# Copying gated products by a transfer into an fp32r tile and transposing them there with an fp32r identity

## What is computed

```python
D_MODEL = 1024; BATCH = 1; SEQ = 256; DEPTH = 2; D_FF = 2816

def swiglu_ffn(x, w_in, w_out):
    gate, up = jnp.split(x @ w_in, 2, axis=-1)
    return (jax.nn.silu(gate) * up) @ w_out

def reference(x, ...):
    for i in range(DEPTH):
        x = x + 0.5 * swiglu_ffn(rms_norm(x, ffn1_norm[i]), ffn1_w_in[i], ffn1_w_out[i])
        xn = rms_norm(x, mix_norm[i])
        ...
        x = x + y
        x = x + 0.5 * swiglu_ffn(rms_norm(x, ffn2_norm[i]), ffn2_w_in[i], ffn2_w_out[i])
    return rms_norm(x, final_norm)
```

## Time and profile before

| | before |
|---|---|
| median of 3 runs | 932.08 us (932.0 to 932.5) |
| the profiled execution | 932.27 us |
| its span, first to last instruction | 930.5 us |
| PE busy | 916.5 us, 98% |
| DVE busy / ACT busy | 525.5 us, 56% / 413.4 us, 44% |
| granted TensorE clock, mean | 0.999 of 2.4 GHz |
| HBM read | 168.63 MB, 182 GB/s |

### The profile page before, as it was taken

One profiled execution on the slowest core, in us unless ns is written; L12 is line 12 of the kernel. 1 busy time (PEld: TensorE's weight loads), 2 busy tenths in 40 slices (PEclk: granted clock), 3 DMA queues, 4 the chain that ended last, 5 costly groups with the idle time before them and its releaser, 6 DMA issues.

```text
span 930.5 us, 11397 instructions
## 1 busy us (share of the span) xinstructions
PE 916.5 (98%) x4349; PEld 764.2 (82%) x4349; DVE 525.5 (56%) x511; ACT 413.4 (44%) x452; POOL 23.6 (3%) x44
## 2 busy tenths in 40 slices
PE   8999999999999999999999999999999999999997
PEld 7888888879878888888878888888799888888885
DVE  5745455458976554453565554545678464454543
ACT  5544344446844442443444434424564263434432
POOL 1400000000000000000000000000000000000000
PEclk9999999999999999999999999999999999999999
DMA  8855646725313856476528465566284266455521
GB/s 279 295 185 181 225 145 206 259 92 189 105 46 118 289 178 207 157 255 240 182 91 267 152 205 190 180 217 213 90 304 149 91 221 231 155 207 180 181 113 46
DMA packets 126668, 170.20 MB, mean 183 GB/s; under 512 B 5237, under 2 KB 111241, under 8 KB 126632
## 3 DMA queue, kind: packets, MB, share of 16 engines
q1 hardware_dynamic: 126632, 169.70, 53.8%
HBM read 168.63 MB, written 1.05 MB: 182 GB/s over the span
## 4 chain that ended last, share of the span: by engine, by line
PE 88%; DVE 7%; ACT 2%; issue 1%; DMA 1%; POOL 0%; SPq 0%; POOLq 0%; ACTq 0%; DVEq 0%
PE ga L962 10%; PE ga L964 10%; PE ga L963 10%; PE ub L964 9%; PE ub L962 9%; PE ub L963 9%; PE acc L962 9%; PE acc L964 9%; PE acc L963 9%; DVE xs L846 3%; DVE w_lo L669 3%; PE tp L1066 2%; PE tp L1023 1%; ACT w_hi L454 1%; DMA raw<-in_ffn_w_in_dram 1%
## 5 line engine op out<-in xcount | busy, mean ns | idle before, releaser
L669 DVE TENSOR_TENSOR w_lo<-raw,w_hi 128x2048 fp32r<-128x2048 f32 (+1 forms) x154 | 349.0, 2290 | 116.2 <-ACT w_hi L454 115.6
L454 ACT ACTIVATE w_hi<-raw 128x2048 fp32r<-128x2048 f32 (+1 forms) x154 | 289.2, 1903 | 30.9 <-DMA raw<-in_ffn_w_in_dram 19.5
L962 PE MATMUL acc<-w_hi,act_hi 128*128 128x512 f32 x416 | 163.5, 393 | 0.0
L964 PE MATMUL acc<-w_hi,act_lo 128*128 128x512 f32 x416 | 162.0, 389 | 0.0
L963 PE MATMUL acc<-w_lo,act_hi 128*128 128x512 f32 x416 | 161.9, 389 | 0.0
L962 PE MATMUL ga<-w_hi,xn_hi 128*128 128x512 f32 x384 | 154.9, 403 | 0.4 <-DVE w_lo L669 0.3
L964 PE MATMUL ga<-w_hi,xn_lo 128*128 128x512 f32 x384 | 150.1, 391 | 0.0
L963 PE MATMUL ga<-w_lo,xn_hi 128*128 128x512 f32 x384 | 149.8, 390 | 0.0
L964 PE MATMUL ub<-w_hi,xn_lo 128*128 128x512 f32 x384 | 149.6, 390 | 0.0
L962 PE MATMUL ub<-w_hi,xn_hi 128*128 128x512 f32 x384 | 149.5, 389 | 0.0
L963 PE MATMUL ub<-w_lo,xn_hi 128*128 128x512 f32 x384 | 149.4, 389 | 0.0
(11 more groups left out here) (133 smaller groups left out, 585.7 us busy)
## 6 DMA issues: line engine op xcount, KB each, us to landing
raw<-in_ffn_w_in_dram SPq DMA_DIRECT2D x176, 512.0 KB, 4.8
raw<-in_ffn_w_out_dram SPq DMA_DIRECT2D x88, 512.0 KB, 4.0
raw<-in_sgu_w_in_dram SPq DMA_DIRECT2D x16, 512.0 KB, 4.5
raw<-in_ab_w_in_dram SPq DMA_DIRECT2D x12, 512.0 KB, 5.0
raw<-in_ab_w_out_dram SPq DMA_DIRECT2D x8, 512.0 KB, 3.9
raw<-in_sgu_w_out_dram SPq DMA_DIRECT2D x8, 512.0 KB, 5.4
gain<-in_ffn_norm_dram SPq DMA_DIRECT2D x4, 512.0 KB, 6.0
xres<-in_x_dram SPq DMA_DIRECT2D x2, 512.0 KB, 5.8
```

The costliest lines, as they stand in the source:

```text
L454: act.activation(w_hi[:, n % RING, o:], raw[:, n % RAW, o:], ACT.Copy).then_inc(hi_split, 1)
L669: dve.tensor_tensor(w_lo[:, n % RING, o:], raw[:, n % RAW, o:], w_hi[:, n % RING, o:].bitcast(F32), ALU.subtract).then_inc(lo_split, 1)
L962: pe.matmul(dst, s_hi, m_hi, start=start, stop=False)
L964: return pe.matmul(dst, s_lo, m_hi, start=False, stop=stop)
```

## The change

- A second identity `ident_r` of type fp32r is made once, by ACT, in the first network.
- `turn` is a pair of fp32r tiles of 128 x 512 in the slots of `act_lo` and `act_hi` that the networks leave free.
- After the two `gate_rows` of steps 0 to 9 ACT runs `to_turn`: it waits until DVE has written both products, waits until the transposes of two steps earlier have read the slot, and issues a transfer of 256 KB from `sgh[:, 1]` to the slot. That is 10 transfers in each network, 40 in all, on ACT's own queue.
- PE waits for the transfer and transposes from the slot with `ident_r`, both operands and the output viewed as fp32r (160 transposes). Step 10 stays as it was (`turned_whole`, 16 transposes).
- The first `product_rows` of steps 1 to 10 waits for the transfer of the step before instead of for its transposes.

```diff
+        ident_r = sb("ident_r", [P, P], F32R)
...
+        turn = [act_lo[:, 6:8, :], act_hi[:, 6:8, :]]
...
+            def to_turn(slot, f, e, i=None):
+
+                act.wait_ge(ga_free, at(f + 1, 2, i))
+                act.wait_ge(ub_free, at(f + 1, 2, i))
+                if e >= 2:
+                    act.wait_ge(hidden_full, at(e - 1, 2, i))
+                act.dma_start(turn[slot].bitcast(F32), sgh[:, 1, :, :]).then_inc(turn_landed, 16)
...
                     gate_rows(1, b, r, f, ACT.Silu)
+                    if k == 0:
+                        act.wait_ge(consts, CONSTS)
+                        act.activation(ident_r[:, :], ident[:, :], ACT.Copy).then_inc(ident_r_ready, 1)
+                    to_turn(0, f, e)
                     split_to(b + 5)
                     with act.Fori(0, (STEPS - 3) // 2) as i:
                         for j in range(2):
...
                             gate_rows(1, n, r + s, f + s, ACT.Silu, i)
+                            to_turn(1 - j, f + s, e + s, i)
                             split(n + 5, i)
...
                         gate_rows(1, n, r + s, f + s, ACT.Silu)
+                        if s < STEPS - 1:
+                            to_turn(s % 2, f + s, e + s)
...
-            def product_rows(t, g, e=0, i=None):
+            def product_rows(t, g, e=0, c=0, i=None):
 
                 if e and t == 0:
                     dve.wait_ge(hidden_full, at(e, 2, i))
+                if c and t == 0:
+                    dve.wait_ge(turn_landed, at(16 * c, 32, i))
...
-                            product_rows(0, g + 2 * s, e + s, i)
-                            product_rows(1, g + 2 * s, e + s, i)
+                            product_rows(0, g + 2 * s, 0, c0 + s, i)
+                            product_rows(1, g + 2 * s, 0, 0, i)
...
-                        product_rows(0, g + 2 * s, e + s)
+                        product_rows(0, g + 2 * s, e + s, c0 + s)
...
-            def turned(bank):
+            def turned(bank, slot, c, i=None):
+
+                pe.wait_ge(turn_landed, at(16 * c, 32, i))
+                for j in range(2):
+                    for t in range(TT):
+                        o = j * T + t * P
+                        mm = pe.transpose(bank[:, o:o + P].bitcast(F32R), turn[slot][:, t, j * P:(j + 1) * P],
+                                          ident_r[:, :])
+                mm.then_inc(hidden_full, 1)
+
+            def turned_whole(bank):
...
                 if kind == "ffn":
                     first_unit(k, f)
+                    pe.wait_ge(ident_r_ready, 1)
...
-                        unit(n, f + 1 + j, i, lambda: turned(tp[j]))
+                        unit(n, f + 1 + j, i, lambda: turned(tp[j], j, c0 + 1 + j, i))
...
-                        turned(tp[(s - 1) % 2])
+                        turned(tp[(s - 1) % 2], (s - 1) % 2, c0 + s)
...
-                    turned(tp[0])
+                    turned_whole(tp[0])
```

More of the change, by code:

```diff
@@ L184, in hybrid_trunk @@
         gated = sem("gated")
+        ident_r_ready = sem("ident_r_ready")
+        turn_landed = sem("turn_landed")
         hidden_full = sem("hidden_full")
@@ L786, in _ @@
                 g = gated0[k]
+                c0 = e // STEPS * (STEPS - 1)
                 if kind == "ffn":
```

## The result

The changed kernel takes 940.18 us, the median of 4 runs (938.52 to 941.96), against 932.12 us for the kernel before. The ratio is 1.0087, with a 95% interval of 1.0073 to 1.0100: it is 8.1 us slower, where 928.3 us and "faster" had been forecast. It is the fastest of the four, so they say less than the whole of the median's loss.

A forecast was written before the change was run, and what follows sets the result against it. The prediction took PE's stream to bound the kernel: -4.8 us of transposes and +1.0 us of waiting gave -3.8, so 928.5 us profiled and 928.3 us as median, with a range of 923.5 to 931.

The forecast's parts named there:

- What bounds the kernel: Whole kernel: PE is busy 916.5 of 930.5 us, so only its stream and its waits change the time.
- The saving: PE's 160 changed transposes: 80 ns each in fp32r instead of 110 in float32, 4.8 us less, between 0 and 6.9.
- the prediction's lower end of 67 ns: Cost of one fp32r transpose if it behaves like wider fp32r matmuls: 53 ns of stream and 13 more.
- The wait at step 0: PE before each network's first transposes, only 24 matmuls after the product: 1.0 us of waiting in all.
- midway between the quiet row and the median of the loaded ones: Assumed landing 3.5 us, between output transfers alone (256 KB, 2.0 to 2.3) and stage 2 slabs (512 KB, 3.8 to 5.9).
- the prediction's own sum for a landing time: Step 0 waits: landing time less 3.1, 3.7, 4.4 and 3.1 us in stages 0, 2, 3 and 5.
- the second rival: Step 0's transfer lands late and PE's wait replaces the saving: slower, 936.6 us at a 5.9 us landing; chance 0.12.
- Step 9: Transfer at step 9: 6.0 us between product and transposes, claimed just enough for the longest landing of 5.9 us.
- ACT, DVE, the raw loads and their rings: Side effects off PE's path: splits and `w_lo` 0.9 us late per steady step, six percent more bytes, no cost.
- The first: Rival: the weight load bounds fp32r transposes at 107 to 120 ns, giving 932.6 to 934.7 us; chance 0.20.
- The third rival: Narrow fp32r transposes need two passes of 107 ns each, making the kernel 16.6 us slower, 949.7 us; chance 0.08.
- The signs named beforehand: Changed profile: transposes near 215 ns, four taking 0.27 to 0.36 us, period 16.62 to 16.73, step 0 waits under 1 us.

The follow-up runs named there:

- the quiet run: Kernel before plus four transfers of the same form and size, issued one after another by ACT at the very end without slabs queued; each landing about 2.3 us.

## Why the prediction was wrong

**What bounds the kernel** held: PE's stream did, and a wait on it cost its full length.

**The saving: right mechanism, about twice too large.** The prediction took 80 ns a transpose and 4.8 us in all. Doubling the groups gave 85 ns against 108 in float32, so the price of one transpose was close. The group saves 0.065 us and not the 0.09 of four times that difference, since 0.03 us are paid once with an fp32r group and 0.01 with a float32 one (periods 16.73 and 16.80, less the 16.36 of the 72 matmuls and four times 85 or 108). The chain puts this down to the next matmul, with 0.30 us for 0.23. The starts say otherwise: that matmul and the one behind it stood 0.32 us apart before and 0.30 apart now, and the distance from the first transpose to the former fell from 0.35 to 0.30 us only. Within the group the starts are 0.06, 0.07, 0.08 and then 0.09 us apart. The transposing loads before them last 139 ns each and start 0.09 us apart. So the first distance is near the prediction's lower end of 67 ns and the later ones fall in with the loads. That the load sets the 85 ns is read from these rows; no run varied it. In place of -4.8 us stands 40 x 0.065 = -2.6.

**The wait at step 0: the term that failed.** The prediction listed the four places and the time that each leaves, 3.1 to 4.4 us, and the windows were right. It then took a landing time of 3.5 us, "midway between the quiet row and the median of the loaded ones since it has half their bytes", and so 1.0 us of waiting. The landings at step 0 were 4.5, 5.7, 4.2 and 5.5 us. By the prediction's own sum for a landing time, stage by stage, that gives 1.4 + 2.0 + 0 + 2.4 = 5.8 us. PE's starts there came 0.6 + 2.2 + 0 + 2.5 = 5.3 us late; in stage 0 the wait for `ident_r` had already taken 0.8. Halving the bytes didn't halve the time: 256 KB in full queues took as long as 512 KB did there, and the same form took 2.3 us alone. With 1 MB less beside it, step 0's transfer came down to 2.3 to 3.6 us. The row of the loaded queues was the one to go by; how the queues share the engines no run shows. The estimate of 2.6 us by the Trainium skill (DMA: Bandwidth & Descriptors, Anatomy of one DMA), which has this fit for transfers issued by GpSimd, is 0.3 us over the 2.3 us of the quiet run, and 1.6 us and more under the landings at step 0. So the second rival occurred, the one that ends slower, given 0.12; its own time for the longest landing, 936.6 us, was passed too, for the most part by the costs named next.

**Step 9** was passed with "just enough for the longest", 6.0 us against 5.9, read in stage 0 only. There and in stage 3 the transfer took 6.0 us and PE just met it. In stage 2 the transfer took 6.6 us, in the kernel with the transfers at the ends 7.0: the longest of four loads was no upper bound.

**Two costs were not in the sum.** PE's idle time brought the clock down to the 1.2 GHz level afterwards, 1.6 us in the profiled run and likely more in the others. And `ident_r` was said to be copied "under ACT's wait in stage 0". The copy stands behind ACT's second gate, and PE asks for it right after its first unit, which that gate follows: 0.8 us of PE's time. The diff shows both places.

**ACT, DVE, the raw loads and their rings: right.** ACT's splits started 1.1 to 1.2 us after its gates in the steady steps, the issue included, where 0.9 had been worked out, and PE's matmuls in the changed kernel waited for no `w_lo`. All 40 transfers with ACT's hold cost 0.04% in an interval of -0.06 to +0.13%.

**The rivals.** The first, the weight load as the bound, did not occur as it was put: the transposing load stayed at 139 ns, as forecast, and the cost is 85 ns and not 107 to 120. Yet a load seems to set these 85. By the rule of the Trainium skill (TensorE: Matmul & The Clock Gate, LDWEIGHTS) 128 columns take 107 ns to load, and the 85 ns measured here don't agree with it. The third rival is out: 160 rows for 160 transposes.

**The signs named beforehand** came as follows. The chain's four transposes took 0.29 us, within 0.27 to 0.36. The transposes' median duration was 245 and 248 ns in the two slots (220 to 283) rather than 215. The period of 16.73 to 16.75 was at the upper edge of 16.62 to 16.73. And waits of over 1.5 us at step 0 were the sign of the second rival.

## What to carry to other kernels

Before moving an operand by a transfer, list for each use how long the consumer leaves between issue and need, and compare the shortest with the longest landing in loaded queues, not with half of it; leave room above that, since 6.6 to 7.2 us came too; use the transfer only where it fits and keep the direct path at the ends. A saving on the bound engine of 0.06 us a step is wiped out by one wait, and the wait can cost the clock on top. A one-time constant belongs ahead of the first work that its maker waits for, and its waits should be looked up on the consumer's side.

## What the runs showed that was not expected

- A transfer of 256 KB within SBUF, on a queue of its own and without HBM, took 2.3 us alone, and beside the slabs on SP's queue a median of 4.5 to 4.8 us in the changed kernel, with 7.2 us where a held slab came with it.
- After PE had idled for 2.3 us the granted clock was 0.51 in the stretch behind it; after 2.0 us in stage 2 of the same run it stayed at 1.00. In the kernel with the transfers at the ends both places lost it. The changed kernel's runs spread over 3.4 us, the longer ones at the lower mean clock, where those of before lie within 0.5.
- Four fp32r transposes of 128 columns added 0.37 us to the 16.36 us of a step's 72 matmuls, eight 0.71: 85 ns each and 0.03 that the group pays once. In float32 four added 0.44 and eight 0.87.
